# Forget and decay gate weights of a hybrid block read in four transfers in place of thirty-two

## What is computed

```python
mod = silu(c) @ w_ada + b_ada              # (6 * 2048): shift, scale, gate, twice
h = rmsnorm(x, g_pre_mix) * (1.0 + scale_m) + shift_m
proj = h @ w_in
fq, fk, fv, ff, gq, gk, gv, ga, gr = split(proj)
log_f = log_sigmoid(ff + b_fgate)          # ff: 8 columns, one per FoX head
log_a = log_sigmoid(ga @ w_gla_a2 + b_gla_a2) / 16   # ga: 16 columns (rank 16)
y = concat([fox(fq, fk, fv, log_f), gla(gq, gk, gv, log_a) * silu(gr)]) @ w_out
x = x + gate_m * rmsnorm(y, g_post_mix)
h = rmsnorm(x, g_pre_mlp) * (1.0 + scale_f) + shift_f
x = x + gate_f * rmsnorm(square(relu(h @ w_mlp_in)) @ w_mlp_out, g_post_mlp)
```

## Time and profile before

| | |
|---|---|
| runs | 2235.6, 2233.84, 2235.53 us |
| median | 2235.53 us |
| span of the profiled execution | 2231.3 us |
| TensorE busy in the span | 2171.6 us, 97% |
| VectorE, ScalarE, GpSimd busy | 1508.8, 868.1, 376.0 us |
| moved by DMA | 441.17 MB, mean 198 GB/s |

### The profile page before, as it was taken

The page is one execution under the profiler, slowest core; times in us unless marked ns, Lnnn a source line. Parts: engine busy times, 40 slices in busy tenths (PEclk is TensorE's granted clock), DMA queues, the critical chain, the costliest instruction groups (busy, mean ns, idle before and its releaser), DMA issues.

```text
span 2231.3 us, 26551 instructions
## 1 busy us (share of the span) xinstructions
PE 2171.6 (97%) x9835; PEld 1765.5 (79%) x9835; DVE 1508.8 (68%) x1485; ACT 868.1 (39%) x1096; POOL 376.0 (17%) x207
## 2 busy tenths in 40 slices
PE   4989999999999999999999999999999999999998
PEld 3568888887777888888888888888878888888886
DVE  6877666666767634664355445544689889898998
ACT  5233333331333223533344335334443444343443
POOL 1000000000000001100000000000035545463645
PEclk9999999999999999999999999999999999999999
DMA  9956554753554353565666656746364765567663
GB/s 363 355 181 215 196 178 142 237 162 113 159 170 137 108 195 101 182 220 215 206 205 220 222 173 205 240 174 203 132 207 170 244 227 169 190 234 244 239 230 147
DMA packets 266403, 441.17 MB, mean 198 GB/s; under 512 B 18156, under 2 KB 118704, under 8 KB 260280
## 3 DMA queue, kind: packets, MB, share of 16 engines
q1 hardware_dynamic: 265472, 435.45, 58.1%
q10 hardware_dynamic: 824, 4.27, 0.5%
HBM read 379.88 MB, written 59.79 MB: 197 GB/s over the span
## 4 chain that ended last, share of the span: by engine, by line
PE 85%; issue 8%; DVE 4%; DMA 1%; ACT 1%; SPq 1%; POOL 0%; DVEq 0%; POOLq 0%; ACTq 0%
PE pair L777 27%; PE pair L779 27%; PE pair L778 26%; DVE am_acc L1880 2%; DMA am_item<-in_w_ada 1%; PE pair L886 1%; PE pair L860 1%; DVE v_op L2165 0%; PE pair L877 0%; PE pair L981 0%; PE pair L926 0%; PE pair L935 0%; PE pair L827 0%; SPq L607 0%; POOL rstd L2330 0%
## 5 line engine op out<-in xcount | busy, mean ns | idle before, releaser
L777 PE MATMUL pair<-in_hi,w_hi 128*128 128x512 f32 (+1 forms) x1800 | 719.6, 400 | 9.2 <-DVE in_lo L2073 3.8
L779 PE MATMUL pair<-in_hi,w_lo 128*128 128x512 f32 (+1 forms) x1800 | 697.2, 387 | 0.0
L778 PE MATMUL pair<-in_lo,w_hi 128*128 128x512 f32 (+1 forms) x1800 | 696.2, 387 | 0.0
L1640 DVE TENSOR_TENSOR w_lo<-w_raw,w_hi 128x2048 fp32r<-128x2048 f32 (+1 forms) x139 | 289.5, 2083 | 395.5 <-ACT w_hi L1207 395.1
L1207 ACT ACTIVATE w_hi<-w_raw 128x2048 fp32r<-128x2048 f32 (+1 forms) x141 | 243.4, 1726 | 466.1 <-PE pair L779 404.8
L777 PEld LDWEIGHTS pair<-in_hi,w_hi 128*128 128x128 f32 x1800 | 339.4, 189 | 88.6 <-issue 20.1
L779 PEld LDWEIGHTS pair<-in_hi,w_lo 128*128 128x128 f32 x1800 | 338.8, 188 | 70.2
L778 PEld LDWEIGHTS pair<-in_lo,w_hi 128*128 128x128 f32 x1800 | 339.6, 189 | 67.6 <-issue 2.6
L777 PE MATMUL pair<-v_op,hid_r 128*128 128x512 f32 x896 | 349.0, 390 | 2.1 <-issue 0.9
L779 PE MATMUL pair<-v_op,hid_r 128*128 128x512 f32 x896 | 348.6, 389 | 0.0
L778 PE MATMUL pair<-v_op,hid_r 128*128 128x512 f32 x896 | 348.6, 389 | 0.0
(11 more groups left out here) (218 smaller groups left out, 1928.9 us busy)
## 6 DMA issues: line engine op xcount, KB each, us to landing
w_raw<-in_w_mlp_in SPq DMA_DIRECT2D x64, 1024.0 KB, 5.3
v_raw<-in_w_mlp_out SPq DMA_DIRECT2D x128, 512.0 KB, 4.9
hid_r<-hid_scratch SPq DMA_DIRECT2D x112, 512.0 KB, 6.3
hid_scratch<-hid_r SPq DMA_DIRECT2D x28, 1792.0 KB, 7.9
am_item<-in_w_ada SPq DMA_DIRECT2D x64, 512.0 KB, 7.6
w_raw<-in_w_in SPq DMA_DIRECT2D x128, 256.0 KB, 3.5
af_item<-in_w_ada SPq DMA_DIRECT2D x64, 512.0 KB, 4.5
w_raw<-in_w_in SPq DMA_DIRECT2D x128, 128.0 KB, 3.6
```

The source lines that it names most:

```text
L777: pe.matmul(dst, a[0], b[0], start=start, stop=False, skip_group_check=onto)
L778: pe.matmul(dst, a[0], b[1], start=False, stop=False, skip_group_check=onto)
L779: return pe.matmul(dst, a[1], b[0], start=False, stop=stop, skip_group_check=onto)
L1640: dve.tensor_tensor(w_lo[n][:, view], w_raw[n][:, view], w_hi[n][:, view].bitcast(F32), ALU.subtract)\
```

## The change

Each half of the gate weights (eight channel tiles) is read with two transfers in place of sixteen. The two halves are issued after item 9 and after item 13, and ScalarE's wait counts 32 in place of 256. The data, their place and the order of everything else stay.

```diff
-            def load_wm(k):
-                if k == 0:
+            def load_wm(half):
+                if half == 0:
                     sp.wait_ge(wm_zero, 1)
-                sp.dma_start(wm_raw[:, k, 0:RANK], w_in_t[:, k, GA_COL:GA_COL + RANK]).then_inc(wm_in[k // 8], 16)
-                sp.dma_start(wm_raw[:, k, 32:32 + FOX_HEADS], w_in_t[:, k, FF_COL:FF_COL + FOX_HEADS]).then_inc(wm_in[k // 8], 16)
+                k = slice(8 * half, 8 * half + 8)
+                sp.dma_start(wm_raw[:, k, 0:RANK], w_in_t[:, k, GA_COL:GA_COL + RANK]).then_inc(wm_in[half], 16)
+                sp.dma_start(wm_raw[:, k, 32:32 + FOX_HEADS], w_in_t[:, k, FF_COL:FF_COL + FOX_HEADS]).then_inc(wm_in[half], 16)
@@
             for n in range(9, 32):
                 load_am(n)
-                if n < 17:
-                    load_wm(2 * n - 18)
-                    load_wm(2 * n - 17)
+                if n in (9, 13):
+                    load_wm((n - 9) // 4)
@@
                 if k in (4, 8):
                     part = slice(2 * k - 8, 2 * k)
-                    act.wait_ge(wm_in[k // 4 - 1], 256)
+                    act.wait_ge(wm_in[k // 4 - 1], 32)
                     act.activation(wm_hi[:, part, :], wm_raw[:, part, :], ACT.Copy).then_inc(wm_hid, 1)
```

## The result

The changed kernel takes 2237.92 us at the median (2235.92 to 2239.59, 20 runs) against 2234.84 us for the kernel before (2233.84 to 2236.01, 20 runs): ratio 1.0015, interval [1.0008, 1.0021]. That is 3.1 us more, between 1.8 and 4.7 by the interval. The median lies within the 0.2% that I had called no change, but the interval excludes zero: the change is a small loss.

A forecast was written before the change was run, and what follows sets the result against it. TensorE, busy for 97% of 2231.3 us, was taken as the bound, with transfer engines full near the edit. Terms -0.2 + 0 + 0.9 = +0.7 us gave span 2232.0, plus 4.2 carried over: 2236.2 us; range 2233.2 to 2239.6.

The forecast's parts named there:

- The likeliest case: Whole kernel: the forecast itself, +0.7 us within 1.5 us, given 52%.
- The third rival: SyncE's queue at each merged pair: engines run empty until the next load flows; +3.8 us, 2239.3 us, 17%.
- The 4.2 us that I carried over: Whole kernel: median of the runs above the profiled span, added to the predicted span of 2232.0 us.
- A shift of the first stage passes on whole: First stage to kernel end: TensorE, busy all the time, passes any shift on; counted in full.
- SyncE's time costs nothing, the engines were full: SyncE's block loads, 36 to 98 us: earlier issues would only queue longer, DMA share 1.09 and 1.06; cost 0.
- The first rival: Items 14 to 16: SyncE's issuing is the limit after all; -3.1 us, 2232.4 us, 14%.
- 28 issues go, 12.6 us of SyncE: SyncE's gate weight issues: 28 fewer at 0.45 us each free 12.6 us of SyncE, costed at nothing.
- Transfer engines, 1.9 us for the old small transfers, of which 0.2 go: Gate weight transfers: 448 of 4608 short packets go; -0.2 us, bounds 0 and -1.7.
- the price goes by the transfer: Gate weight transfers: rival in which the engines' 1.9 us shrink to 0.2; -1.7 us, 2233.8 us, 13%.
- Order, 0 at the end: Items 14 to 16: more small transfers ahead, item 15 0.5 us later, swallowed by item 22's wait; 0, at worst 0.5 us.
- Holding of the queue, +0.9 us: SyncE's queue behind each merged pair: 0.45 us dry time each, two pairs +0.9 us, bounds 0 and +2.5.
- the marks that I had set for the profile: Changed profile: holds 1 to 4 us, share 1.05 except dips, items 14 to 16 0.3 to 1.5 us later, block 3 under 1.5.

The follow-up runs named there:

- e2: Against the kernel before: half 0 merged into two transfers behind item 9, half 1 left in sixteen; 2236.08 us, +1.2 us, interval 0.9997 to 1.0015.
- e3: Against the kernel before: half 1 merged into two transfers behind item 13, half 0 left in sixteen; 2237.94 us, +3.1 us.
- e8: Kernel before with all thirty-two gate weight transfers left out, both gates coming from zeros; 2232.61 us, -2.1 us.
- e1: Kernel before with its thirty-two small transfers moved, sixteen behind item 9 and sixteen behind item 13; 2242.22 us, +7.3 us.
- e7: Changed kernel's merged transfers issued from ScalarE, behind modulation of channel tiles 3 and 7, instead of SyncE; 2234.36 us, -0.4 us over the kernel before.
- e4: Kernel before with sixteen transfers of two tiles each (256 pieces) at the same places, replacing thirty-two; 2235.83 us, +0.9 us, interval 0.9994 to 1.0012.
- e5: Against the kernel before: half 1 merged into two transfers behind item 20, half 0 left in sixteen; 2235.80 us, +1.1 us.
- e12: The kernel before run again unchanged, for a second profile; 2235.01 us, -0.6 us over the kernel before, interval 0.9988 to 1.0011.

## Why the prediction was right, and where it was off

The measured 2237.9 us lies in the range, 1.7 us above the forecast 2236.2. As a difference the miss is larger: +3.1 us measured against +0.7 forecast. Part of the closeness is luck, since the three runs of the kernel before that I started from have a median 0.7 us above that of its twenty. The likeliest case (+0.7 us within 1.5) did not come. The third rival, the queue that runs dry behind the big ones (+3.8 us, 17%), did, with its place and nearly its size, and the number is right because the range was drawn wide enough to hold it. Its split was another: it gave each pair 1.75 us, where e2 and e3 have +1.2 us (not told from zero) and +3.1 us.

The 4.2 us that I carried over from the profile to the runs are not all time around the span. Each later profiled execution has its time on record (2239.31 us for the span of 2237.5), and there it is 1.8 us. The first profile of the kernel before was thus itself some 2.4 us shorter than the median of its three runs. The forecast doesn't suffer, being that median plus 0.7 us.

- *A shift of the first stage passes on whole*: held. Block 3 moves by 4.4 us in a profile whose block 1 moved by 4.1. It reaches the end as well: measured from 117.0, the mean of the two profiles of before, the shift of block 3 and the difference of the medians agree within 1.2 us in all twelve other profiles, from e8 (-1.7 and -2.1 us) to e1 (+6.6 and +7.3 us).
- *SyncE's time costs nothing, the engines were full*: held. e7 and e8 take all gate weight issues from SyncE, and item 14 starts 0.6 to 0.7 us sooner. The first rival (up to -3.1 us) is excluded by e7's item 14.
- *28 issues go, 12.6 us of SyncE*: wrong in itself. The four transfers and the issues behind them hold SyncE for 8.0 + 8.2 = 16.2 us; the thirty-two took 14.4 (32 x 0.45, by the medians). It did no harm to the sum, where this time had no price, but it is the root of the next point.
- *Transfer engines, 1.9 us for the old small transfers, of which 0.2 go*: e8 gives 2.1 us for all (0.2 to 4.2 by the interval, SyncE's issues included), which fits but is no close test. The part of 0.2 is too small to be seen. The rival "the price goes by the transfer" is not seen in e4, which has half as many.
- *Order, 0 at the end*: the 0.5 us at item 15 fit e5, where half 1 no longer stands ahead of items 14 to 16 and item 14 comes 0.5 us sooner. That they cost 0 at the end no run shows by itself.
- *Holding of the queue, +0.9 us*: this is the step that failed, in size: +0.9 us, bounds 0 and +2.5, where the runs show about 3 us. I let the queue shrink to what it takes (80 pieces per engine), and counted from there one issue and one start-up, at most 1.25 us a pair and 0.45 as the likeliest. That the hand-over itself has a rate was named only in the rival, from `ada`. The trace of before held the figure: L617 and L618 issue 128 pieces in 0.45 us, so 1024 would take 3.6 us. With it a pair is 7 us and more. In the changed kernel the last transfer in front of the second pair landed 9.2 us after its issue at 50.39, so at 59.6 (row below); SyncE was through with the pair at 59.35, and what it issued then needed another microsecond to flow. e2 and e3 show the two pairs apart, +1.2 and +3.1 us.

```profile
DMA to landing us min/median/max: 7.8/8.5/9.2
```

- *The Trainium skill* (DMA: Bandwidth & Descriptors, "Anatomy of one DMA") has it that many descriptors can be emitted before the cost shows up. That sentence is about GpSimd's path; on SyncE's here, the second 1024 short pieces of a pair hold it for 2.3 to 4.1 us (e3 and the changed kernel), so the measurement decides against using it. The Trainium skill's advice to coalesce (same page, "Rules for kernel authors") brought nothing, since the pieces stayed as many.

Of the marks that I had set for the profile, two came true: two second transfers held for about 4 us, and dips near 45 and 58 us. The others failed. Items 14 to 16 were 3.7 to 4.3 us late and not 0.3 to 1.5, the sum of block 3 moved by 4.4 us and not by less than 1.5, and the share outside the dips was under 1.05 (1.02 in 66:98, the third dip in it). The share was under 1 from 58 to 64 us, so by my own sign ("under 1 for more than 2 us") the mechanism of the likeliest case was wrong, though the number fell into the range.

## What to carry to other kernels

Merging transfers saves little if the contiguous runs stay as many: here SyncE pays some 0.35 to 0.5 us per 128 runs of 32 or 64 bytes (2.7 to 3.9 ns each), whether they come in one transfer or in eight. What merging does change is that the hand-over comes in one piece, so before doing it compare its whole length (runs x 3.5 ns, from these runs) with the work that the queue holds at that place, and put it where nothing urgent is behind it, or on another engine's queue. And here an engine that issued 3.3 us late was hardly a limit while the DMA share stood at its full value (1.09), although the chain of waits ran through its issues.

## What was not expected of the hardware

The rate of hand-over was one thing: 2048 short pieces take 5.5 to 10.0 us of SyncE in two, four or sixteen transfers, while the two `ada` transfers of 4096 runs of 512 bytes were through in 9.1 us, 2.2 ns each. Why a short run costs more is open; those runs are contiguous on the SBUF side (8 KB per partition), ours are not (a step of 160 bytes), and that was not tried apart.

The other is the granted clock. TensorE stands idle for 5.4 us before the sum of block 3 in both kernels (the earlier trace rows and above). In that idle time the granted clock falls to half, that is 1.2 GHz in place of 2.4 (0.66 in 114:116 and 0.50 in 116:118 before), and it stays there for a time that differs from profile to profile. Stretches before, then after (the third value from the end is the clock):

```profile
120.00:122.00 2.00, 2.00 (x7) 1.61 (x6) 1.76 (x6) 1.28 (x2) 0.00 (x0) 0.64 1.10 351
122.00:124.00 2.00, 2.00 (x10) 1.64 (x10) 1.85 (x4) 1.50 (x3) 0.00 (x0) 1.00 1.01 321
```

```profile
126.00:128.00 2.00, 2.00 (x6) 1.52 (x6) 1.85 (x3) 1.89 (x3) 0.00 (x0) 0.50 1.02 327
128.00:130.00 2.00, 2.00 (x9) 1.60 (x8) 2.00 (x3) 0.00 (x0) 0.00 (x0) 0.85 0.10 34
```

Before, it is back at full some 4.6 us after the sum at 116.86 (0.64 in 120:122); after, 7.3 us after the sum at 121.25 (0.85 in 128:130). The second profile of the kernel before has 7.7 us, so this is no difference of the two kernels. The profiles with 7.3 to 7.7 us (both of the changed kernel, and e12) have 31.7 to 31.9 us from that sum to the first gate sum, those with about 5 us (before, e1, e3, e5) 29.9 to 30.7, and the other seven lie between (5.3 to 6.2 us, 30.8 to 31.2 us). So it is worth some 1.4 us of a single profile, as much as several of the effects studied here, and may be part of why the intervals are wide; what sets its length was not tested.
